# Three reorderings in a two-block network's kernel: a copy ahead of a sigmoid, a later slab split in the scan, an FFN whose first tiles are fed one by one

## The reference

```python
for l in range(2):                                 # first block
    x = x + 0.5 * swiglu_ffn(x, ...)               # 1024 -> 2816 -> 1024
    h = rms_norm(x, mix_norm[l])
    y_a, y_b, y_c = diff_attention(...), chunk_attention(...), retention(...)
    g = sigmoid(gates)                             # three gates of width 1024
    x = x + (g0*(y_a@w_a) + g1*(y_b@w_b) + g2*(y_c@w_c)) @ w_out[l]
    x = x + 0.5 * swiglu_ffn(x, ...)
# second block: a state-space scan in both directions, then an FFN
hx = rms_norm(x) * (1 + scale) + shift
y  = ssd_bidir(...) + xs * d_skip
y  = rms_norm(y * silu(z), g_ssd)
x  = x + gm * rms_norm(concat(fourier_mix(u), y) @ w_out, g_post_mix)
hx2 = rms_norm(x, g_pre_ffn) * (1 + scale) + shift
x  = x + gf * rms_norm((silu(hx2 @ w_gate) * (hx2 @ w_up)) @ w_down, g_post_ffn)
```

## Time and profile before

| | us |
|---|---|
| median of three runs | 1623.92 |
| lowest and highest run | 1622.88, 1626.29 |
| the profiled execution, its own time | 1624.92 |
| its span, from the first to the last instruction | 1622.4 |
| TensorE busy | 1607.2 (99%) |
| VectorE busy | 1293.1 (80%) |
| ScalarE busy | 923.2 (57%) |
| GpSimd busy | 210.2 (13%) |

### The profile page before, as it was taken

The page is one execution under the profiler, slowest core; times in us unless marked ns, Lnnn a source line. Parts: engine busy times, 40 slices in busy tenths (PEclk is TensorE's granted clock), DMA queues, the critical chain, the costliest instruction groups (busy, mean ns, idle before and its releaser), DMA issues.

```text
span 1622.4 us, 29880 instructions
## 1 busy us (share of the span) xinstructions
PE 1607.2 (99%) x13136; PEld 1541.8 (95%) x13136; DVE 1293.1 (80%) x1463; ACT 923.2 (57%) x1096; POOL 210.2 (13%) x122
## 2 busy tenths in 40 slices
PE   8999999999999999999999999999999999999998
PEld 8999988999999999999987899999999989899998
DVE  8887878687889888897878688885999597796655
ACT  7554655684465455545556686464655567554544
POOL 1000100000040001200000000032323368400000
PEclk9999999999999999999999999999999999999999
DMA  8667654444566765776754444555555434235552
GB/s 296 229 259 279 246 181 168 146 155 158 214 229 235 269 250 199 267 260 254 282 184 165 147 157 156 185 219 191 190 201 182 145 118 155 79 131 190 200 186 75
DMA packets 47520, 317.56 MB, mean 196 GB/s; under 512 B 5280, under 2 KB 8096, under 8 KB 9888
## 3 DMA queue, kind: packets, MB, share of 16 engines
q1 hardware_dynamic: 47248, 315.64, 53.3%
q10 hardware_dynamic: 144, 0.02, 0.0%
HBM read 314.60 MB, written 1.05 MB: 195 GB/s over the span
## 4 chain that ended last, share of the span: by engine, by line
PE 82%; DVE 9%; ACT 4%; POOL 2%; DMA 1%; issue 1%; SPq 0%; DVEq 0%; ACTq 0%
PE ps L1170 23%; PE ps L1172 23%; PE ps L1171 23%; PE ps L1368 3%; PE ps L1370 3%; PE ps L1369 3%; DVE wlo L1844 2%; ACT whi L648 1%; DVE pre L2455 1%; DMA raw<-in_w_dram 1%; PE ps L1382 1%; DVE dA_rows L1844 1%; DVE tmp L1844 1%; PE ps L1393 1%; DVE qkA L1844 1%
## 5 line engine op out<-in xcount | busy, mean ns | idle before, releaser
L1844 DVE TENSOR_TENSOR wlo<-raw,whi 128x2048 fp32r<-128x2048 f32 (+1 forms) x256 | 585.0, 2293 | 92.8 <-ACT whi L648 89.3
L648 ACT ACTIVATE whi<-raw 128x2048 fp32r<-128x2048 f32 (+1 forms) x264 | 499.9, 1905 | 216.9 <-DMA raw<-in_w_dram 216.9
L1170 PE MATMUL ps<-h1hi,whi 128*128 128x256 f32 x1792 | 500.8, 279 | 2.9 <-DVE wlo L1844 2.9
L1172 PE MATMUL ps<-h1lo,whi 128*128 128x256 f32 x1792 | 496.7, 277 | 0.0
L1171 PE MATMUL ps<-h1hi,wlo 128*128 128x256 f32 x1792 | 496.6, 277 | 0.0
L1170 PEld LDWEIGHTS ps<-h1hi,whi 128*128 128x128 f32 x1792 | 337.0, 188 | 7.1 <-issue 4.2
L1172 PEld LDWEIGHTS ps<-h1lo,whi 128*128 128x128 f32 x1792 | 337.1, 188 | 0.0
L1171 PEld LDWEIGHTS ps<-h1hi,wlo 128*128 128x128 f32 x1792 | 336.8, 188 | 0.1
L1170 PE MATMUL ps<-hid_hi,whi 128*128 128x256 f32 x880 | 244.0, 277 | 0.0
L1172 PE MATMUL ps<-hid_lo,whi 128*128 128x256 f32 x880 | 243.4, 277 | 0.0
L1171 PE MATMUL ps<-hid_hi,wlo 128*128 128x256 f32 x880 | 243.4, 277 | 0.0
(11 more groups left out here) (363 smaller groups left out, 2536.5 us busy)
## 6 DMA issues: line engine op xcount, KB each, us to landing
raw<-in_w_dram SPq DMA_DIRECT2D x288, 1024.0 KB, 4.8
raw<-in_w_dram SPq DMA_DIRECT2D x8, 256.0 KB, 5.4
c_rows<-in_c_rows_dram SPq DMA_DIRECT2D x2, 1024.0 KB, 9.9
relbias<-in_relbias_dram SPq DMA_DIRECT2D x2, 1024.0 KB, 8.5
pv<-in_pv_dram SPq DMA_DIRECT2D x2, 641.0 KB, 7.5
xT<-in_x_dram SPq DMA_DIRECT2D x4, 256.0 KB, 4.6
raw<-in_w_dram SPq DMA_DIRECT2D x2, 512.0 KB, 7.1
ctxT<-in_ctx_dram SPq DMA_DIRECT2D x1, 1024.0 KB, 6.9
```

What stands on the lines that cost most here:

```text
L648: act.activation(whi[:, slot, c], raw[:, slot, c], ACT.Copy).then_inc(hi_done[slot], 1)
L1170: pe.matmul(out, w_hi, hi, start=start, stop=False, skip_group_check=skip)
L1172: return pe.matmul(out, w_hi, lo, start=False, stop=stop, skip_group_check=skip)
L1844: return dve.tensor_tensor(out, a, b, op)
```

## The change

Three places are touched.

1. In each layer, ScalarE copies `pT` of stage WB0 before the sigmoid of `tmp`, not after it.
2. In the scan, VectorE splits output slab 1 after `within_weights(2)`, not after `within_weights(0)`, and makes the low half of u_t after the loop, not before `carried_scale(3)`.
3. In block 2's last FFN, slab FFN30 is split by VectorE ahead of the first `gated_x`, not by GpSimd. Tile 6 of `sq` is added on VectorE, and TensorE's column sum of it is gone. The first scaling and adding of x are done for tile 0 alone ahead of the second root, and the scaling has moved behind the variance. The first pair goes tile by tile: TensorE starts on tile 0 with both slabs when `h_lo_ready` says so, then on tile 1.

```diff
@@ gpsimd
         cut_lo(b2 + WOUT20 + 3)
-        cut_lo(b2 + FFN30)
@@ scalar
             cut_hi(m + 27)
+            evacuate(WB0, pT[:, 0:8, :], 1024, 3072)
             act.wait_ge(cg_low, l + 1)
             sigmoid(tmp[:, 0, :]).then_inc(cg_sig, 1)
-            evacuate(WB0, pT[:, 0:8, :], 1024, 3072)
@@ tensor, ffn
-            for j in range(4):
-                pe.wait_ge(h_lo_ready, 4 * n + j + 1)
+            for k in range(2 if n == NF3 else 0):
+                pe.wait_ge(h_lo_ready, 4 * n + k + 1)
+                for half in range(2):
+                    slot = weights(g0 + half)
+                    for c in range(2):
+                        block3(ps[:, 4 + half, c * S:(c + 1) * S], slot, c * KT + k, h_hi[:, k, :], h_lo[:, k, :],
+                               start=(c == 0 and k == 0), stop=False, skip=True)
+            for j in range(1 if n == NF3 else 0, 4):
+                pe.wait_ge(h_lo_ready, 4 * n + j + (2 if n == NF3 else 1))
@@ tensor, sums
-        for v, k in ((0, 0), (0, 6), (0, 7), (1, 0), (1, 6), (2, 0), (2, 6), (1, 7), (2, 7)):
+        for v, k in ((0, 0), (0, 7), (1, 0), (1, 6), (2, 0), (2, 6), (1, 7), (2, 7)):
             out_sum(v, k)
@@ vector
         for e in range(4):
-            if e == 3:
-                ycat_low(0, 0, u_t[:, :, :])
             carried_scale(e)
             within_weights(e)
             if e == 0:
                 z_clamp(1)
-                cut_lo(b2 + WOUT20 + 1)
             if e == 1:
                 z_clamp(2)
+            if e == 2:
+                cut_lo(b2 + WOUT20 + 1)
+        ycat_low(0, 0, u_t[:, :, :])
@@ vector, after the output product's inputs
+        cut_lo(BLOCK2_0 + FFN30)
         gated_x(0, 2)
@@
-        folded(sq).then_inc(out_folded, 1)
+        done(folded(sq))
+        dve.wait_ge(sq2_ready, 7 + 7)
+        tt_(sq[:, 0, :], sq[:, 0, :], sq[:, 6, :], ALU.add).then_inc(out_folded, 1)
@@
-        done(mix_scale(0))
         dve.wait_ge(sum2_done, SUMS2[3])
...
-        done(mix_add(0))
+        done(mix_scale(0, 1))
+        done(mix_add(0, 1))
         norm2_end(3)
-        for j in range(4):
+        for k in range(2):
+            scaled_tile(k, affn, gx_ready, r3)
+            if k == 0:
+                done(mix_scale(1, 1))
+                done(mix_add(1, 1))
+        hx_tile(0, 3 * KT, KT).then_inc(h_lo_ready, 1)
+        done(mix_scale(2, 2))
+        hx_tile(1, 3 * KT, KT).then_inc(h_lo_ready, 1)
+        done(mix_add(2, 2))
+        for j in range(1, 4):
             x_scaled(j, affn, gx_ready, r3)
             if j < 3:
-                done(mix_scale(j + 1))
+                done(mix_scale(2 * j + 2, 2))
             hx_low(j, 3 * KT, KT, h_lo_ready)
             if j < 3:
-                done(mix_add(j + 1))
+                done(mix_add(2 * j + 2, 2))
```

More of the change, by code:

```diff
@@ L2414, in norm2, with scaled_tile @@
             norm2_end(k, width)
+        def scaled_tile(k, gain, signal, r):
+            c = slice(k % 2 * S, (k % 2 + 1) * S)
+            dve.scalar_tensor_tensor(gx[:, k // 2 % 2, c], xT[:, k, :], gain[:, k:k + 1], r[:, :],
+                                     ALU.mult, ALU.mult).then_inc(signal, 1)
         def x_scaled(j, gain, signal, r):
[L2418 to L2421, removed]
-        def hx_low(j, first, count, signal):
[L2425 to L2429, removed]
+            for k in (2 * j, 2 * j + 1):
+                scaled_tile(k, gain, signal, r)
+        def hx_tile(k, first, count):
+            c = slice(k % 2 * S, (k % 2 + 1) * S)
+            dve.wait_ge(hx_hi_ready, count + k + 1)
+            return dve.scalar_tensor_tensor(hlo[:, k, :], gx[:, k // 2 % 2, c], mods[:, first + k, 0:1],
+                                            hhi[:, k, :].bitcast(F32), ALU.add, ALU.subtract)
+        def hx_low(j, first, count, signal):
+            for k in (2 * j, 2 * j + 1):
+                ins = hx_tile(k, first, count)
             ins.then_inc(signal, 1)
@@ L2597, in _, with mix_scale @@
         folded(mix_xg).then_inc(out_folded, 1)
-        def mix_scale(j):
-            g = mix_g[:, 2 * j:2 * j + 2, :]
-            return tt_(g, g, r2[:, :].unsqueeze(1).to_broadcast([P, 2, S]), ALU.mult)
+        def mix_scale(k, n):
+            g = mix_g[:, k:k + n, :]
+            return tt_(g, g, r2[:, :].unsqueeze(1).to_broadcast([P, n, S]), ALU.mult)
         gated_x(6, 1)
@@ L2612, in _, with mix_add @@
         dve.scalar_tensor_tensor(var2[:, :], rsqb[:, :], 1.0 / D, x_var, ALU.mult, ALU.add).then_inc(var2_ready, 1)
-        def mix_add(j):
-            x2 = xT[:, 2 * j:2 * j + 2, :]
-            return tt_(x2, x2, mix_g[:, 2 * j:2 * j + 2, :], ALU.add)
-        done(mix_add(0))
-        norm2_end(3)
-        for j in range(4):
+        def mix_add(k, n):
+            x2 = xT[:, k:k + n, :]
+            return tt_(x2, x2, mix_g[:, k:k + n, :], ALU.add)
+        done(mix_scale(0, 1))
+        done(mix_add(0, 1))
+        norm2_end(3)
+        for k in range(2):
[8 more added lines that the diff above has]
+        for j in range(1, 4):
             x_scaled(j, affn, gx_ready, r3)
             if j < 3:
-                done(mix_scale(j + 1))
+                done(mix_scale(2 * j + 2, 2))
             hx_low(j, 3 * KT, KT, h_lo_ready)
             if j < 3:
-                done(mix_add(j + 1))
+                done(mix_add(2 * j + 2, 2))
         done(dve.memset(rscale[:, :], 1.0))
```

## The result

| us | kernel before | changed kernel |
|---|---|---|
| median, first comparison | 1623.89 (20 runs) | 1626.58 (20 runs, 1625.29 to 1634.34) |
| median, second comparison | 1623.88 (35 runs) | 1626.02 (12 runs, 1624.96 to 1632.16) |
| profiled execution, own time | 1624.92 | 1632.75, and 1626.03 in the second |
| its span | 1622.4 | 1631.0, and 1624.2 |

The ratio is 1.0025, 95% interval [1.0017, 1.0033], and in the second comparison 1.0018 [1.0003, 1.0032]. The forecast was 1626.5 us, +2.6 us on the median; measured are +2.7 and +2.1 us. The executions of the changed kernel form two groups: 23 of 32 from 1625.0 to 1627.3 us and 9 from 1631.1 to 1634.3 us, at a granted clock of 0.999 to 1.000 in all of them. The first profiled execution is of the upper group. So it is read together with the second one.

What follows compares the result with a forecast made beforehand. TensorE's own work at full clock was taken to bound nearly the whole span of 1622.4 us. Terms -0.6 + 2.5 + 0.7 = +2.6 us gave a median of 1626.5 us (profiled 1627.5); range 1622.0 to 1629.0 us.

Steps and rivals of the forecast that it cites:

- copies, both layers: pT copy before the sigmoid: TensorE's waits of 0.35 and 0.32 us go; -0.6 us, bounds -0.7 and 0.
- scan: Moved split and low half of u_t stand behind GpSimd, y's chain starts later; +2.5 us, bounds -1.25 and +2.6.
- last FFN up to the end of the pairs: Block 2's last FFN: early start becomes a stop one pair later; +0.7 us, bounds -0.5 and +1.1.
- rival 4: Layer copies: something else held L1503, so the copy does not help; +0.6 us on the forecast; within the rest, 0.06.
- The 0.32 us of the earlier trace: Layer 2: TensorE's stand of 0.32 us before its pT matmul, taken as the copy's and counted as -0.3 us.
- The choice between the 1.28, 1.34 and 2.09 us and the one split that lost nothing: Scan: VectorE operations held up beside GpSimd, giving +2.5 us, against a split at 1370.14 that lost 0.15, giving +0.2 us.
- Rival 1: Scan: the engines do not exclude each other for moved split and low half; -1.2 us, 1622.7 us; chance 0.15.
- rival 2: Scan: low half of u_t gets between GpSimd's two halves; total +2.0 us, 1625.9 us; chance 0.2.
- The head: Last FFN: with the first pair by tiles and scaling behind the variance, TensorE starts 0.47 us earlier, at 1431.3.
- The later pair: Last FFN: pair 1's hlo ends at 1435.2 instead of 1434.53; TensorE stops 1.1 us one pair later.
- "nothing" for the split of FFN30: Last FFN: VectorE's 2.28 us split fits a 4.37 us hole; mix_xg saves 1.4 us but the next operation waits anyway.
- Rival 3: TensorE's stops between 1394 and 1405 lower its granted clock; 2.8 us more, 1629.3 us; chance 0.07.

Runs made afterwards that it cites:

- e2: The kernel before with only the scan's part of the change; median 1625.92 us, ratio 1.0010 [0.9993, 1.0028].
- e3: The kernel before with only the last FFN's part of the change; median 1623.31 us, ratio 1.0001 [0.9988, 1.0014].
- e5: The changed kernel, but GpSimd splits output slab 3 only after the third z product of y's chain; 1626.16 us, ratio 1.0015 against the kernel before.
- e6: The changed kernel with the low half of u_t back ahead of the scaling of e=3; 1629.25 us, ratio 1.0035 against the kernel before.
- e1: The kernel before with only the copy moved ahead of the sigmoid; median 1626.96 us, ratio 1.0020 [1.0006, 1.0035].

## Why the prediction was right, step by step

| step | forecast | measured on TensorE |
|---|---|---|
| copies, both layers | -0.6 | -0.4 (rows: -0.43 and -0.18, less 0.22) |
| scan | +2.5 | +2.67, +2.56, +2.64 in three traces |
| last FFN up to the end of the pairs | +0.7 | +0.42, +0.22, +0.40, +0.20 in four |
| sum | +2.6 | +2.5; medians +2.7 and +2.1 |

That the sum is met within 0.1 us is in part luck: the copies were put 0.2 us too good and the last FFN 0.4 us too dear. The scan is the term that was worked out right.

- **The copy.** The wait at L1503 is gone in both layers, and rival 4 falls. The size was over-stated: 343 to 352 us is 0.42 or 0.43 us shorter with the copy moved, in each of the eleven traces that have it, but 0.24 and 0.21 us shorter in the two traces (e2, e3) that do not have it, so that about 0.2 us belongs to it there; in layer 2 it is 0.17 or 0.18 us. The 0.32 us of the earlier trace rows was misread: that row is a weight load, and in all eleven traces the same load still starts 0.13 us after the one before it, with nothing to wait for. Only 0.19 us of the 0.32 were the copy's. The profile of before is at fault for the rest: it has its gate slabs from 347 to 375 us at 117.8 ns, every later trace has them at 113.3 ns behind 353 us. This also makes three steps of -0.2 us, 48 matmuls by 4.5 ns, that have no edit behind them, and it flattered every kernel compared with that one trace by 0.8 us.
- **The scan.** Each link held. The first turning is at 1378.68 in the first trace, which is 1.14 us ahead at the scan's start: 1379.82 on the clock of before, as forecast. The clamp takes 2.49 us until GpSimd's first half is over, the split 3.15 us (forecast 3.2), the last turning comes at +0.84 us against the scan's start (forecast +0.75), the low half takes 2.63 us, y's chain starts at +2.68 us (forecast +2.54). The choice between the 1.28, 1.34 and 2.09 us and the one split that lost nothing was the step on which all hung; e5 confirms it by taking GpSimd away, and e6 adds who goes first. The trace agrees with the Trainium skill ("SBUF — State Buffer", section "Who interferes with whom"), by which the two exclude each other for a whole instruction where VectorE's has two inputs in SBUF, as the split and the low half have. Rival 1 needed a split that ends before 1388.3 and a short low half; rival 2 needed the low half between the halves. Neither is seen in any of the traces with the split moved.
- **The last FFN.** The head: TensorE's first matmul moved from +1.18 us (VectorE's second mix_xg, 1414.22 for 1413.04 in the second profile) to +0.72 us, -0.46 us for the forecast -0.47. The later pair: hlo of pair 1 at 1435.49 for 1433.65, +0.66 us against the same base for the forecast +0.67; TensorE's stop is 0.98 us (forecast 1.1). Of the four totals in the table the two of 0.4 us have the second half of the pairs' 96 matmuls at 117.8 ns, the two of 0.2 us at 113.3 ns: 0.2 us of pace. The mis-sized term is another: "nothing" for the split of FFN30. TensorE was at +1.6 us when the sums began, VectorE only at +1.18 us. In the kernel before, the mix_xg that stood 2.09 us behind GpSimd is followed by one that starts 1.28 us after ScalarE began the mix_g pair it needs; in the changed kernel it starts 0.93 to 0.94 us after (rows behind this list). That 0.35 us hid most of the added tile 6, and the part cost about 0.3 us, not 0.7. It comes with the split on VectorE in all nine traces that have it there and in none of the five that don't; no run moves the split alone, so that the split is its cause is likely and not shown.
- **Rival 3.** No drop of the clock is in the scan of the changed kernel's two traces, whose stops are at most 1.3 us; the three stops that the rival named (1.1, about 2 and 1.1 us) are 1.11, 0.30 and 0.94 us. But the mechanism is real here. In the scan the clock fell to 0.50 at a stop of 1.83 us (e1) and one of 3.98 us (e6), and did not at five stops of 1.35 to 1.76 us; its price was 1.6 and 2.6 us. At the start of e2 it also fell, from 7.9 to 11.3 us, behind a stop of 2.01 us. Whether the change, by cutting the 1.76 us stop, made a drop less likely is not shown: each case is one execution.
- **Not foreseen.** The upper group, 5 to 7 us above. It lies outside the range; the median hardly sees it (1626.2 and 1626.0 us without that group).

The rows for the second mix_xg, in the kernel before and in the second profile of the changed kernel:

```profile
1411.76 0.83 ACT L1093 ACTIVATE mix_g<-ps,small 128x256 f32<-128x256 f32 x2
1413.04 0.69 DVE L1844 TENSOR_TENSOR mix_xg<-xT,mix_g 128x512 f32<-128x512 f32 x1 [0.98 <-ACT mix_g L1093]
```

```profile
1413.28 0.83 ACT L1092 ACTIVATE mix_g<-ps,small 128x256 f32<-128x256 f32 x2
1414.22 0.69 DVE L1850 TENSOR_TENSOR mix_xg<-xT,mix_g 128x512 f32<-128x512 f32 x1 [2.03 <-ACT mix_g L1092]
```

## What to carry over

Before an operation is moved, write GpSimd's queue beside VectorE's, with times: two operations that cost nothing on their own can each stand for the other's full length, and the one that pays most here is the last short one in front of the critical chain. A kernel with a stop of TensorE of nearly 2 us can lose 1.6 us more in some executions: the same stop on yoff, in the same code, took 1.35 to 1.83 us in the six traces that have it, and the clock fell in one. A single trace at full clock does not show that it always stays there. And a single profiled execution of "before" carries 0.8 us of its own; compare stage by stage with several traces before a term of 0.3 us is believed.

## What the hardware showed that I had not expected

- Matmuls of 128x256 start 113.3 or 117.8 ns apart at the same granted clock of 1.00. The level changes where TensorE stops or does matmuls of another shape, with one exception in these traces (at 14 us in e1). 4.5 ns are 6.6 us over the last FFN.
- Between VectorE and GpSimd the one that has waited longer goes first, even if the other's next instruction follows its last one directly: 2.82 us for an operation of 0.68 us (e6).
- Where the first mix_xg stood behind GpSimd, the second starts 0.35 us later after its input's producer than it does elsewhere: 1.28 to 1.29 us in five traces with that hold, against 0.93 us in nine without. The cause isn't known, and it is no rule: behind the held operations of the scan the next one starts at once.
- TensorE's granted clock fell to 0.50 after a stop of 1.83 us, when TensorE had been at work again for 1.4 us, and stayed at 1.00 after one of 1.76 us; each was seen in one execution.
